# Three edits of order in a retention and convolution backbone: who computes the last norm, where two weight splits stand, which tile is centred first

## The reference

```
p   = modulate(x, sh1, sc1) @ w_in                      # q, k, v, g, a, b
o   = retention(q, k, v) forward + backward             # 8 heads of 64
ret = silu(g) * (groupnorm(o) * gn_w + gn_b)            # per head
conv= silu(layer_norm(depthwise31(a * sigmoid(b))))     # 512 channels
x   = layer_norm(ALPHA * x + g1 * (concat(ret, conv) @ w_out), ln1_w, ln1_b)
h   = square(relu(modulate(x, sh2, sc2) @ w_ff1))
x   = layer_norm(ALPHA * x + g2 * (h @ w_ff2), ln2_w, ln2_b)
```

## Time and profile before

| | us |
|---|---|
| median of 3 runs (lowest to highest) | 2862.11 (2859.53 to 2862.59) |
| the profiled execution, its own time | 2868.7 |
| its span, first to last instruction | 2866.9 |
| PE busy, share of the span | 95% |
| DVE, POOL, ACT busy | 68%, 37%, 26% |
| mean granted TensorE clock | 0.975 |

### The profile page before, as it was taken

The page is one execution under the profiler, slowest core; times in us unless marked ns, Lnnn a source line. Parts: engine busy times, 40 slices in busy tenths (PEclk is TensorE's granted clock), DMA queues, the critical chain, the costliest instruction groups (busy, mean ns, idle before and its releaser), DMA issues.

```text
span 2866.9 us, 38099 instructions
## 1 busy us (share of the span) xinstructions
PE 2711.5 (95%) x13644; PEld 2234.2 (78%) x13644; DVE 1937.4 (68%) x3216; ACT 735.6 (26%) x1521; POOL 1074.9 (37%) x1077
## 2 busy tenths in 40 slices
PE   6999999799999999999999699998889999999996
PEld 3778879578888888888888588887677888888885
DVE  4699993758776776677668799873665454454456
ACT  3233334536111111111111523334533111111111
POOL 1344454755121212121212745564763333333335
PEclk8999999799999999999999899999899999999998
DMA  8322322631122222222220312212511111111111
GB/s 243 99 86 76 103 77 75 189 103 38 59 74 73 73 73 73 73 73 73 74 38 30 107 46 63 63 49 69 162 63 52 44 44 58 45 44 51 51 44 66
DMA packets 246659, 214.69 MB, mean 75 GB/s; under 512 B 60385, under 2 KB 203281, under 8 KB 246545
## 3 DMA queue, kind: packets, MB, share of 16 engines
q1 hardware_dynamic: 149488, 120.94, 14.1%
q10 hardware_dynamic: 97056, 92.29, 10.5%
HBM read 190.56 MB, written 22.63 MB: 74 GB/s over the span
## 4 chain that ended last, share of the span: by engine, by line
PE 82%; DVE 6%; POOL 5%; DMA 2%; issue 2%; ACT 2%; SPq 1%; ACTq 0%; DVEq 0%; POOLq 0%
PE bank L651 15%; PE bank L653 15%; PE bank L652 15%; PE bank L1218 9%; PE bank L1219 9%; PE bank L1220 9%; PE bank L756 1%; PE bank L1074 1%; PE bank L1076 1%; PE bank L1075 1%; PE bank L1151 1%; PE bank L1125 1%; PE bank L1136 1%; PE bank L1150 1%; POOL w_lo L647 1%
## 5 line engine op out<-in xcount | busy, mean ns | idle before, releaser
L1674 POOL TENSOR_TENSOR w_lo<-raw,w_hi 128x1024 fp32r<-128x1024 f32 x120 | 288.1, 2402 | 1111.5 <-ACT w_hi L1496 1111.5
L1218 PE MATMUL bank<-x_hl,w_hi 128*128 128x512 f32 (+1 forms) x1280 | 476.6, 372 | 10.2 <-DVE x_hl L1712 10.2
L1219 PE MATMUL bank<-x_hl,w_hi 128*128 128x512 f32 (+1 forms) x1280 | 472.7, 369 | 0.0
L1980 DVE TENSOR_TENSOR work<-work,bank 128x512 f32<-128x512 f32 x576 | 390.0, 686 | 122.4 <-PE bank L653 111.5
L1220 PE MATMUL bank<-x_hl,w_lo 128*128 128x512 f32 (+1 forms) x1280 | 472.4, 369 | 0.0
L1956 DVE TENSOR_TENSOR work<-work 128x512 f32<-128x512 f32 (+1 forms) x160 | 156.4, 978 | 450.4 <-ACT work L1484 449.5
L651 PE MATMUL bank<-w_hi,h_hi 128*128 128x512 f32 x1152 | 450.1, 391 | 6.8 <-DVE work L1980 5.3
L653 PE MATMUL bank<-w_hi,h_lo 128*128 128x512 f32 x1152 | 448.4, 389 | 0.0
L652 PE MATMUL bank<-w_lo,h_hi 128*128 128x512 f32 x1152 | 448.3, 389 | 0.0
L1858 DVE SCALAR_TENSOR_TENSOR bank<-work,bank 128x512 f32<-128x512 f32 (+1 forms) x580 | 406.9, 701 | 17.8
L1496 ACT ACTIVATE w_hi<-raw 128x1024 fp32r<-128x1024 f32 x120 | 126.8, 1059 | 776.7 <-PE bank L653 584.2
(11 more groups left out here) (143 smaller groups left out, 4421.8 us busy)
## 6 DMA issues: line engine op xcount, KB each, us to landing
raw<-in_w_ff ACTq DMA_DIRECT2D x128, 512.0 KB
work<-in_w_ada SPq DMA_DIRECT2D x48, 512.0 KB
plain_words<-in_w_ada ACTq DMA_DIRECT2D x64, 256.0 KB
raw<-in_w_in SPq DMA_DIRECT2D x60, 256.0 KB
plain_words<-in_w_ada SPq DMA_DIRECT2D x16, 512.0 KB, 11.8
raw<-in_w_out SPq DMA_DIRECT2D x10, 512.0 KB
gate_rows<-work SPq DMA_DIRECT2D x72, 64.0 KB, 1.6
retention_rows<-work SPq DMA_DIRECT2D x72, 64.0 KB, 1.6
```

The costliest lines, as they stand in the source:

```text
L1218: nc.tensor.matmul(o, slot(mlp_slot(l, f), 0)[:, wc], x_hi[:, k, cols], start=k == 0, stop=False)
L1219: nc.tensor.matmul(o, slot(mlp_slot(l, f), 0)[:, wc], x_lo[:, k, cols], start=False, stop=False)
L1674: nc.gpsimd.tensor_tensor(slot(mlp_slot(l, sl), 1), raw[:, un % 2, :], slot(mlp_slot(l, sl), 0).bitcast(F32), ALU.subtract).then_inc(w_rea ...
L1980: nc.vector.tensor_tensor(X[:, t, hc], X[:, t, hc], gated, ALU.add).then_inc(S["y_read"], 1)
```

## The change

Layer 1's second norm: tiles 0, 1, 2, 6 and 7 are made whole by DVE, tiles 3, 4 and 5 in the common way (before: 6 and 7, and 0 to 5). The semaphore counts that used to be tile numbers now count the tiles made in the common way (`kept`, `kept_of`); POOL's root of tile st waits, where tile st - 2 is whole, until DVE has scaled that tile. The list of layer 1's last block becomes hidden 0, 1, 2, share 0, 1, 2, hidden 3, share 3 to 7; layer 0's stays. In both layers DVE takes the statistics of the new tile ahead of the step on the tile before. In both layers' mix stages the splits of units 4 and 5, on ACT and on POOL, move from steps 1 and 2 to steps 4 and 5, and DVE centres tile 1 between `variance(0)` and `scale_heads(0)`.

```diff
--- before.py
+++ after.py
@@ -101,7 +101,18 @@
 
 def whole_by_vector(layer, ln, j):
 
-    return ln == "ln2" and j >= len(tiles_of(layer)) - (2 if layer == DEPTH - 1 else 1)
+    n = len(tiles_of(layer))
+    return ln == "ln2" and (j < 3 or j >= n - 2 if layer == DEPTH - 1 else j == n - 1)
+
+
+def kept(layer, ln, j):
+
+    return sum(not whole_by_vector(layer, ln, i) for i in range(j + 1))
+
+
+def kept_of(layer, ln, j, odd):
+
+    return sum(i % 2 == odd and not whole_by_vector(layer, ln, i) for i in range(j + 1))
 
 
 def last_kind(group):
@@ -706,7 +717,8 @@
             for ci, (t0, nt) in enumerate(chunks):
                 shares = [("share", T.index(t)) for t in range(t0, t0 + nt)]
                 following = [("hidden", 2 * ci + 2 + f) for f in range(2) if ci + 1 < len(chunks)]
-                seq += following[:1] + shares[:2] + following[1:] + shares[2:]
+                first = 3 if l else 2
+                seq += following[:1] + shares[:first] + following[1:] + shares[first:]
             return seq
 
         def by_vector(ln, j):
@@ -1288,7 +1300,7 @@
             def normalise(l, ln, j):
 
                 t = tiles_of(l)[j]
-                act.wait_ge(S[ln + "_shift"], BEFORE[l][ln + "_shift"] + j + 1)
+                act.wait_ge(S[ln + "_shift"], BEFORE[l][ln + "_shift"] + kept(l, ln, j))
                 nc.scalar.activation(X[:, t, :], X[:, t, :], ACT.Identity, bias=shift[:, j % 2, :], scale=rs[:, j % 2, :]).then_inc(S[ln + "_act"], 1)
 
             def load(l, u):
@@ -1456,8 +1468,8 @@
                         act.wait_ge(S["cn_shift"], s0["cn_shift"] + j + 1)
                         nc.scalar.activation(X[:, T[j], 512:D], banks[4 + j % 2][:, :], ACT.Identity,
                                              bias=shift[:, j % 2, :], scale=rs[:, j % 2, :]).then_inc(S["cnorm"], 1)
-                    if st in (1, 2):
-                        load(l, IN_UNITS + 3 + st)
+                    if st in (4, 5):
+                        load(l, IN_UNITS + st)
                 load(l, IN_UNITS + 6)
                 load(l, IN_UNITS + 7)
                 load(l, IN_UNITS + OUT_UNITS)
@@ -1623,8 +1635,8 @@
                         nc.gpsimd.tensor_tensor(rs[:, st % 2, :], mv[:, st % 2, 1:2], neg_half[:, 0:1], ALU.pow).then_inc(S["cn_pow"], 1)
                         pool.wait_ge(S["gn_var"], s0["gn_var"] + st + 1)
                         nc.gpsimd.tensor_tensor(gstat[:, st % 2, 2 * HEADS:], gstat[:, st % 2, HEADS:2 * HEADS], neg_half[:, 0:HEADS], ALU.pow).then_inc(S["gn_pow"], 1)
-                    if st in (1, 2):
-                        split_low(pool, l, IN_UNITS + 3 + st)
+                    if st in (4, 5):
+                        split_low(pool, l, IN_UNITS + st)
                 for u in range(6, 10):
                     split_low(pool, l, IN_UNITS + u)
 
@@ -1633,18 +1645,20 @@
                     for st in range(n + 2):
                         if st < n:
                             pool.wait_ge(S[ln + "_var"], s0[ln + "_var"] + st + 1)
-                            if st >= 2:
-                                pool.wait_ge(S[ln + "_act"], s0[ln + "_act"] + st - 1)
+                            if st >= 2 and not whole_by_vector(l, ln, st - 2):
+                                pool.wait_ge(S[ln + "_act"], s0[ln + "_act"] + kept(l, ln, st - 2))
+                            elif st >= 2:
+                                pool.wait_ge(S["ln2_whole"], s0["ln2_whole"] + st - 1 - kept(l, ln, st - 2))
                             nc.gpsimd.tensor_tensor(rs[:, st % 2, :], mv[:, st % 2, 1:2], neg_half[:, 0:1], ALU.pow).then_inc(S[ln + "_pow"], 1)
                         if st >= 2 and not whole_by_vector(l, ln, st - 2):
                             j = st - 2
                             xt = X[:, T[j], :]
                             if by_vector(ln, j):
-                                pool.wait_ge(S[ln + "_x"], s0[ln + "_x"] + sum(by_vector(ln, i) for i in range(j + 1)))
+                                pool.wait_ge(S[ln + "_x"], s0[ln + "_x"] + kept_of(l, ln, j, 1))
                             else:
-                                pool.wait_ge(S[ln + "_act"], s0[ln + "_act"] + j + 1)
+                                pool.wait_ge(S[ln + "_act"], s0[ln + "_act"] + kept(l, ln, j))
                                 nc.gpsimd.tensor_tensor(xt, xt, ln_rows[:, 0, :], ALU.mult).then_inc(S[ln + "_own"], 1)
-                                pool.wait_ge(S[ln + "_own"], s0[ln + "_own"] + j // 2 + 1)
+                                pool.wait_ge(S[ln + "_own"], s0[ln + "_own"] + kept_of(l, ln, j, 0))
                             nc.gpsimd.tensor_tensor(xt, xt, ln_rows[:, 1, :], ALU.add).then_inc(done, 1)
                         if ln == "ln" and l and st in (1, 4):
                             gate_weights(0, u0 + 2 + (st > 1))
@@ -1739,7 +1753,7 @@
             def ln_weight(l, j, ln, ln_rows):
 
                 if by_vector(ln, j):
-                    dve.wait_ge(S[ln + "_act"], BEFORE[l][ln + "_act"] + j + 1)
+                    dve.wait_ge(S[ln + "_act"], BEFORE[l][ln + "_act"] + kept(l, ln, j))
                     xt = X[:, tiles_of(l)[j], :]
                     nc.vector.tensor_tensor(xt, xt, ln_rows[:, 0, :], ALU.mult).then_inc(S[ln + "_x"], 1)
 
@@ -1910,11 +1924,12 @@
                 link(nc.vector.memset(sq[:, :, DK:], EPS))
                 centre(0)
                 variance(0)
+                centre(1)
                 scale_heads(0)
                 for st in range(1, n + 4):
                     if st >= 4:
                         combine(st - 4)
-                    if st < n:
+                    if 1 < st < n:
                         centre(st)
                     if 2 <= st <= n:
                         scale_heads(st - 1)
@@ -2014,15 +2029,17 @@
                     elif p < len(seq):
                         ti = seq[p][1]
                         share(NBLK - 1, False, [ti])
+                    if p < len(seq) and seq[p][0] == "share":
+                        dve.wait_ge(S["y_read"], s0["y_read"] + (NBLK - 1) * YB + 2 * (ti + 1))
+                        if ti >= 2 and whole_by_vector(l, "ln2", ti - 2):
+                            dve.wait_ge(S["ln2_pow"], s0["ln2_pow"] + ti - 1)
+                        row_stats(ti % 2, T[ti], S["ln2_var"])
                     if 0 < p <= len(seq) and seq[p - 1][0] == "share":
                         if whole_by_vector(l, "ln2", seq[p - 1][1]):
                             dve.wait_ge(S["ln2_var"], s0["ln2_var"] + seq[p - 1][1] + 1)
                             whole_centre(l, seq[p - 1][1])
                         else:
                             ln_shift(l, seq[p - 1][1], "ln2")
-                    if p < len(seq) and seq[p][0] == "share":
-                        dve.wait_ge(S["y_read"], s0["y_read"] + (NBLK - 1) * YB + 2 * (ti + 1))
-                        row_stats(ti % 2, T[ti], S["ln2_var"])
                     if p > 1 and seq[p - 2][0] == "share":
                         if whole_by_vector(l, "ln2", seq[p - 2][1]):
                             whole_scale(l, seq[p - 2][1])
```

## The result

| | before | after |
|---|---|---|
| median of 7 runs (lowest to highest) | 2862.59 (2857.2 to 2863.98) | 2869.77 (2866.27 to 2872.35) |
| the profiled execution, its own time | 2868.7 | 2872.32 |
| its span | 2866.9 | 2870.5 |
| mean granted TensorE clock | 0.975 | 0.973 |

The ratio is 1.0020, 95% interval 1.0011 to 1.0030: slower, by 3 to 9 us.

The account below looks back on a forecast made before the run. It took PE to bound 82% of the span, with changes only where the chain leaves PE. Mix stages +2.1, layer 0's end 0 and tail +0.3 gave +2.4 us: 2871.1 profiled, 2864.5 median, range 2858.5 to 2868.

Parts of the forecast that it names:

- The end of layer 0's last block: Layer 0's last block: only the order of statistics and 128x1 step changes; cost 0, bounds -0.4 and +1.6 us.
- the roots: Early centring of tile 1: DVE would not wait for POOL's root; by the skill's rule, some 0.9 us more per layer.
- The mix stage: Both layers' mix stages: ramp -2.29 us, splits at steps 4 and 5 +3.35; +1.06 us per layer, +2.1 in all.
- without a change in what PE does: Mix-stage ramp: L1613 of tile 3 comes 2.29 us earlier, the 13.11 us behind tile 1's transposes staying; bounds -1.5 and -4.2.
- rival (a): Ramp gains its bound, splits fall into POOL's gaps, -2.5 us per layer; half the tail's meetings; 2855.3 us, chance 0.08.
- (b): Mix stages: ramp gives nothing at tile 3, splits cost in full, 3.35 us per layer; 2869.1 us, chance 0.12.
- Rival (c): Mix stages: DVE's wide instructions wait for POOL's roots too, 0.9 us more per layer; 2866.3 us, chance 0.10.
- The last norm: Layer 1's tail: DVE's last five wide instructions meet POOL twice, ending at 2863.9; +0.3 us, bounds -4.0 and +4.2.
- The order edit: Layer 1's last norm: three 128x1 steps behind the statistics, 0.12 us each, 0.4 us of DVE work.
- the last subtraction: Whole kernel: the median taken as 6.6 us below the profiled execution, turning 2871.1 into 2864.5 us.

Follow-up runs that it names:

- e2: The kernel before with only layer 0's last block in the new order (statistics ahead of the step on the old tile): 2866.12 us, ratio 1.0012.
- e13: The changed kernel with only the order of step and statistics undone, in both layers: 2865.14 us, ratio 1.0007 to the kernel before.
- e9: The kernel before with two 128x1 DVE instructions added ahead of DVE's weight of tile 5 in layer 0's last block: 2865.14 us, ratio 1.0008.
- e10: The changed kernel with one more POOL root ahead of POOL's bias of tile 4 in layer 0's last norm: 2866.16 us, ratio 1.0013 to the kernel before.
- e1: The changed kernel with the old order back in layer 0's last block only: 2865.92 us, ratio 1.0008 to the kernel before.
- e5: The changed kernel with ACT's hidden-step ReLU issued ahead of the pending normalisation in layer 0: 2869.33 us, ratio 1.0018 to the kernel before.
- e8: The changed kernel with the old order at one place only, tile 3's share in layer 0's last block: 2867.03 us, ratio 1.0010 to the kernel before.
- e6: The kernel before with only layer 1's last norm dealt out anew and its list changed: 2862.67 us, ratio 0.9991.
- e7: e1 with the two splits apart, POOL's at step 2 and behind the last tile, ACT's at steps 2 and 5: 2861.6 us, ratio 0.9990 to the kernel before.
- e3: The kernel before with only the two weight splits moved to steps 4 and 5: 2868.43 us, ratio 1.0016.
- e14: The same kernel as e3, timed again: 2864.55 us, ratio 1.0006 to the kernel before.
- e4: The kernel before with only tile 1 centred ahead of tile 0's scaling: 2864.42 us, ratio 1.0001.
- e11: e6 with early centring and the two splits apart (POOL step 2 and behind the last tile): 2858.27 us, ratio 0.9984 to the kernel before.
- e12: e11 without the early centring of tile 1: 2859.24 us, ratio 0.9988 to the kernel before.

## Why the prediction was wrong

The failed step is the one headed "The end of layer 0's last block": "Cost 0; bounds -0.4 [...] and +1.6". It measured +3.36 us (98.33 less 94.97), twice its upper bound, and e2 and e13 pin it to that edit. The argument had been that POOL is the engine without gaps, its inputs come long before, and DVE's weight of tile 7 ends with POOL's instruction whenever it starts. It looked at the one weight that already met POOL and not at the weight of tile 5, which started 0.17 us ahead of POOL's bias. The row for the price of that meeting was at hand: 3.24 us in the tail. The upper bound took the 1.6 us of the later step as the worst that could be passed on; in this meeting what was passed on was nearly the other engine's whole instruction, 2.03 us of POOL's 2.35.

The Trainium skill, page "SBUF — State Buffer", section "Who interferes with whom", puts it as "Issue order, not op shape, decides who blocks". By that rule, the trace agrees: with the same two instructions, e9 and e10 each turn it round. The prediction used this section for the roots and did not apply it to the edit that changes an order.

The mix stage: mechanism right, size off. From centre 0, L1613 of tile 0 came 0.59 us later (forecast 0.61), that of tile 3 3.22 us earlier (32.88 and 29.66; forecast 2.29, bound 4.2), and from tile 3 to the last 3.81 us were added (44.64 and 48.45; forecast 3.35, bound 3.75). The ramp gave more than the value "without a change in what PE does", and the split took 2.88 us from DVE's L1907 where its row of the ramp had 2.82. In layer 1 tile 3 came 3.30 us earlier (33.63 and 30.33) and 3.78 were added. Together +0.59 and +0.48 instead of +1.06 each. One pair of profiles says this too finely: the six kernels with this mix stage (after, e1, e5, e8, e10, e13) have 78.07 to 78.93 and 63.02 to 64.00, on average 78.31 and 63.48, against 77.50 and 62.68 for the four with the old one. By these the stage costs 0.8 us in each layer, and the forecast was nearer than the pair makes it look. The ramp lies about halfway between the forecast's 2.29 and rival (a)'s 4.2, but none of (a)'s splits is in POOL's gaps; (b) fails at tile 3.

Rival (c) fell: the centring at 517.02 took 0.69 us inside the root.

The last norm: the layout held. DVE ran its last five wide instructions with two meetings that it paid for (2858.20 and the first L1737, now L1751), POOL getting in between two of them; no wait for a root. The tail is 44.61, not 45.4: PE stalled for 0.74 us (forecast 1.0), and POOL's bias met DVE's L1731 (now L1745) at 2856.94 and paid itself. The order edit, of which the prediction counted 0.4 us here, costs 0.72 (43.89 in e13). The new deal alone is worth -1.2 us (43.90 against 45.12, e6): the only part of the change that gains.

On the profiled time the sum was 2871.1 and the execution took 2872.32, an error of 1.2 us: +3.36 for the failed step, -0.47 and -0.58 for the mix stages, -0.81 for the tail, and -0.3 in the rest. On the median the error is 5.3 us. The other 4 us come from the last subtraction: the profile of before happened to lie 6.1 us over its median, the profile of after lies 2.6 over its own. That offset belongs to an execution, not to a kernel: in the experiments it ran from -3.5 us (e9, e7) to +4.8 (e10). Without the failed step the median would have been about 2866.4 us, without the error of the offset about 2865.7; either lies inside the range, so it took both to miss it. In ratios the offset drops out: forecast +0.08%, measured +0.20%, and +0.07% in e13, where the order is undone. That agreement is in part luck: by its stages e13 is level with the kernel before (-0.04 us), since the mix stages and the tail came out lower than forecast, and its interval runs from -0.02 to +0.16%. Of the 7.2 us between the medians the profiles show 3.6; the ratio's interval reaches down to 3.1, and the separately timed parts (e2 0.12%, e3 and e14 0.16 and 0.06%, e4 0.01%, e6 -0.09%) sum to 0.10 to 0.20%, without the order in layer 1. Whether the medians hold some us that no stage shows is open.

## What to carry to other kernels

When an edit shifts two engines against each other by tenths of a microsecond, list every pair of wide instructions of theirs that start within 0.5 us of one another, and price each at the full swing (here 1.22 or 3.25 us), not at the shift. Put extra work of a helper engine where its partner's short critical instruction doesn't follow, or behind the loop: with one split at step 2 and the other behind the loop's work the mix stages of e7, e11 and e12 were 2 to 3 us shorter per layer; moved together to steps 4 and 5 they cost about 1 us in layer 0. And take an edit apart into stages on the profile before adding its terms: errors of opposite sign hid the failed step in the total.

## What the hardware showed that was not expected

A swing of 2.03 us hung on 0.37 us: DVE 128x1024 with two inputs from SBUF takes 1.22 us when it starts 0.17 us ahead of POOL's instruction of that size and 3.25 us when it starts 0.17 or 0.18 us behind it (e9, after); POOL takes 3.25 or 3.10 instead of 2.35 when it is second (before, e10). POOL's 128x8 root of 1.65 us did not hold up a DVE instruction of 0.69. And one root of 0.55 us put into POOL's queue shortened the stretch by 1.07 us. The same first products of layer 1 ran fifteen matmuls in 4 us at a granted clock of 1.00 in the kernel before, and ten at 0.57 in e10; the waits just ahead of them were 1.84 and 2.35 us, and what set the clock is open.
